# Weight slots requested from a recorded plan, first uses cast into the rings, and norm chains placed behind FFN matmuls, in a two-layer decoder trunk on eight cores

## The chip, the cores and the metric

The kernel runs as one program on all 8 cores of a Trainium2 chip. Each core takes half of one of the 4 sequences (4096 tokens and 128 more of overlap, 4224 in all), and no core waits for another. The time is device microseconds of the slowest core. Before the change it is 5761.13 us, the median of 6 runs from 5758.85 to 5765.34 us.

## The reference

Two layers; `d` is 1024, the FFN width 2816, the memory 256 tokens. Shortened from the reference:

```python
for l in range(2):
    x = x + 0.5 * swiglu(rms_norm(x, ffn1_norm[l]), gate1[l], up1[l], down1[l])      # F1
    h = rms_norm(x, mix_norm[l])
    q, k, v, u = split(h @ w_in[l])                          # 512 | 128 | 128 | 512 columns
    out_a = sliding_window_sink_attention(rope(q), rope(k), v, sinks[l])   # window 128, 8 heads
    out_b = multiscale_pool(u, pool_w[l], pool_scale[l])     # trailing means over 2, 4, 8, 16
    x = x + concat(rms_norm(out_a), rms_norm(out_b)) @ w_out[l]
    x = x + cross_attention(rms_norm(x), rms_norm(mem), wq[l], wkv[l], wo[l])   # 4 heads
    x = x + 0.5 * swiglu(rms_norm(x, ffn2_norm[l]), gate2[l], up2[l], down2[l])      # F2
return rms_norm(x, final_norm)
```

All weights arrive as f32 in HBM.

## The kernel before

The activations lie with the 1024 channels on the partitions (8 chunks of 128) and the tokens along the free dimension. The 4224 tokens are cut into nine tiles, six of 512 and three of 384, and each is passed twice, once for each layer: 18 passes. The main loop has 20 visits, `v` from -1 to 18. Visit `v` weaves three jobs together: F2 of pass `v-1`, the mixer and the cross attention of pass `v` (together M), and F1 of pass `v+1`. Visit -1 has F1 of pass 0 alone, visit 0 has no F2, visit 17 no F1, visit 18 only F2. In visits 0 and 9 M also prepares the memory (`memkv_steps`): it folds the memory's keys and values with `wq` and `wo` into eight slots `wab`, which the cross attention of the layer then reads.

The order of the work is written out by hand as lists of closures. `merge` weaves two lists by weights, `sprinkle` spreads one list evenly through another, and `run` calls the closures. Each call emits instructions to five in-order queues (PE, DVE, ACT, POOL, SP), and semaphores make one engine wait for another. In a visit with all three jobs the order is:

- gate and up of F2 (`gu2`, 22 pairs of 16 matmuls and an eviction), woven with the norm, the input projection and the pooling of M (`seg1`);
- down of F2 (`dn2`, 8 outputs of 22 matmuls), woven with the windowed attention (`seg2`) and with the norm that F1 needs (`prenorm_steps`); `seg2` ends with the norm of the attention's output (`ast.fin`, `anorm`);
- gate and up of F1 (`gu1`), woven with the output projection (`segw`);
- down of F1 (`dn1`): its first 72% with the cross attention (`seg4`), the rest with the norm for the next F2 (`tail`).

A norm is a chain over four engines: ACT squares a chunk, POOL adds it up, after the eighth chunk PE multiplies the sum by ones (`ps<-sb_ach,sb_ones` in the rows), ACT takes Ln and Exp (`sb_rst`), and DVE writes the scaled chunks into `sb_hF` or `sb_hM`, which PE then reads.

Weights come in slots of 128 x 2048 bf16 (512 KB; 16 matmuls of 512 columns use one) through two rings: F with six buffers (`sb_fr`), M with four (`sb_mr`). `load` issues a slot's DMA where the slot is first used in program order. The casts from f32 are DMAs of the POOL queue. The first use of F1's weights of layer 0 (`wf` 0, 33 slots, visit -1) casts straight into the ring, and SP writes the bf16 back to HBM (`wfb`). All other weights are first converted HBM to HBM: `conv_first` (the 9 slots of `wm` and the 16 of `wx`, layer 0) runs between visits -1 and 0, `conv_second` (`wf` 1) is sprinkled through visit 0, and layer 1's weights through visits 1 to 7.

The softmax here doesn't subtract the row's maximum and nothing guards it: scores larger than these inputs give would overflow.

## Time and profile before

| | |
|---|---|
| median of 6 runs | 5761.13 us |
| the profiled execution's own time | 5766.19 us |
| its span, first to last instruction, slowest core (core 6) | 5764.6 us |
| spans of all cores | 5731.9 to 5764.6 us |
| PE busy | 5175.1 us, 90% of the span |
| DVE, ACT, POOL busy | 2318.4, 1633.0, 937.1 us |
| HBM read, written | 1017.94 MB, 142.74 MB |
| chain that ended last | PE 75%, DVE 7%, DMA 7%, ACT 4%, issue 4% |

An engine's share is an average over visits with different limits, so the visits are looked at one by one. Their borders are read from the evictions of F1 and F2: visit -1 ends with the eighth down eviction at 265.6 us, visit 0 at 723.4 us, visit 1 at 1038.9 us. Where PE has no gap, an idle engine elsewhere costs nothing.

### The profile page before, as it was taken

What the parts mean: (1) busy time and instruction counts of PE and PEld (TensorE: products, weight loads), DVE (VectorE), ACT (ScalarE), POOL (GpSimd) and SP (SyncE); (2) the same over time, 40 slices, a digit from 0 to 9 for tenths busy, and PEclk for the clock granted to TensorE, in tenths of its full rate; (3) what the DMA queues carried; (4) which work ended last, traced back from release to release, by engine and by line L of the source; (5) the groups of instructions that cost most, each with busy time, mean ns of one, the idle gap of its engine ahead of it and who ended that gap; (6) DMA issues with size and microseconds to landing.
All of it is one profiled execution on the core that took longest, in us unless ns stands there. A gap on an engine that the chain in (4) does not pass through costs nothing.

```text
span 5764.6 us, 79056 instructions; the slowest of 8 cores (5731.9 to 5764.6 us)
## 1 busy us (share of the span) xinstructions
PE 5175.1 (90%) x25851; PEld 2493.6 (43%) x25851; DVE 2318.4 (40%) x3800; ACT 1633.0 (28%) x2824; POOL 937.1 (16%) x1015
## 2 busy tenths in 40 slices
PE   6436699999999999999999889999999999999988
PEld 2113244444444444455545434444444444455545
DVE  2122253444444443434434335353434444344452
ACT  1104232222323232222222333232232323232342
...
GB/s 192 124 149 162 170 174 202 154 200 150 189 162 181 170 194 176 198 211 230 201 188 160 178 174 142 162 136 179 132 176 136 167 143 173 161 187 182 196 157 165
DMA packets 254044, 991.79 MB, mean 172 GB/s; under 512 B 29264, under 2 KB 29664, under 8 KB 251008
## 3 DMA queue, kind: packets, MB, share of 16 engines
...
q10 hardware_dynamic: 1152, 2.10, 0.1%
...
HBM read 1017.94 MB, written 142.74 MB: 201 GB/s over the span
## 4 chain that ended last, share of the span: by engine, by line
PE 75%; DVE 7%; DMA 7%; ACT 4%; issue 4%; POOL 1%; another core or an unknown queue 1%; DVEq 0%; ACTq 0%; POOLq 0%; SPq 0%
PE ps L335 75%; DMA sb_fr<-wf 2%; DVE sb_hF L435 2%; DVE sb_hM L435 2%; DMA sb_fr<-wfb 1%; ACT sb_rst L148 1%; DMA wab<-sb_mr 1%; ACT sb_tmp L148 1%; DVE sb_x L523 1%; DMA sb_mr<-wmb 1%; DVE sb_hM L777 1%; DMA wfb<-sb_fr 1%; POOL sb_acc L407 1%; ACT sb_pT L148 1%
## 5 line engine op out<-in xcount | busy, mean ns | idle before, releaser
L335 PE MATMUL ps<-sb_hF,sb_fr 128*128 128x512 bf16 (+1 forms) x12672 | 2679.4, 367 | 172.2 <-DVE sb_hF L435 78.0
L335 PEld LDWEIGHTS ps<-sb_hF,sb_fr 128*128 128x128 bf16 x12672 | 1247.8, 99 | 1500.0 <-issue 303.3
L335 PE MATMUL ps<-sb_act,sb_fr 128*128 128x512 bf16 (+1 forms) x6336 | 1355.0, 366 | 95.3 <-DMA sb_fr<-wf 66.6
L487 DVE TENSOR_TENSOR sb_act<-ps,sb_sg 128x512 bf16<-128x512 f32 (+1 forms) x792 | 510.7, 645 | 1637.5 <-PE ps L335 1353.9
L407 POOL TENSOR_TENSOR sb_acc<-sb_acc,sb_sqf 128x512 f32<-128x512 f32 (+2 forms) x534 | 632.2, 1187 | 2482.6 <-ACT sb_sqf L148 2460.3
L335 PEld LDWEIGHTS ps<-sb_act,sb_fr 128*128 128x128 bf16 x6336 | 621.8, 99 | 760.1 <-issue 154.5
L335 PE MATMUL ps<-sb_hM,sb_mr 128*128 128x512 bf16 (+1 forms) x3600 | 832.5, 370 | 127.6 <-DMA sb_mr<-wmb 79.2
L148 ACT ACTIVATE sb_sg<-ps 128x512 f32<-128x512 f32 (+1 forms) x792 | 438.8, 558 | 1045.2 <-PE ps L335 909.9
L148 ACT ACTIVATE sb_sqf<-sb_x 128x512 f32<-128x512 f32 (+1 forms) x567 | 330.4, 591 | 991.1 <-DVE sb_x L825 432.9
L335 PEld LDWEIGHTS ps<-sb_hM,sb_mr 128*128 128x128 bf16 x3600 | 356.1, 99 | 539.4 <-issue 208.9
L148 ACT ACTIVATE sb_pT<-ps 128x512 bf16<-128x512 f32 (+2 forms) x436 | 232.3, 567 | 472.8 <-PE ps L335 472.1
L523 DVE SCALAR_TENSOR_TENSOR sb_x<-ps,sb_x 128x512 f32<-128x512 f32 (+1 forms) x288 | 183.9, 639 | 200.8 <-PE ps L335 200.7
L335 PE MATMUL ps<-sb_pT,sb_mr 128*128 128x512 bf16 (+2 forms) x1280 | 259.8, 354 | 3.2 <-DMA sb_mr<-wxb 3.0
L948 DVE TENSOR_TENSOR sb_pT<-sb_pT,sb_tmp 128x512 bf16<-128x512 bf16 (+1 forms) x144 | 103.4, 759 | 354.4 <-ACT sb_tmp L148 327.4
L435 DVE SCALAR_TENSOR_TENSOR sb_hF<-sb_x,sb_vecs,sb_rst 128x512 bf16<-128x512 f32 (+1 forms) x288 | 203.2, 761 | 46.4 <-ACT sb_rst L148 46.4
L435 DVE SCALAR_TENSOR_TENSOR sb_hM<-sb_x,sb_vecs,sb_rst 128x512 bf16<-128x512 f32 (+1 forms) x288 | 182.4, 701 | 55.9 <-ACT sb_rst L148 55.9
L976 DVE TENSOR_TENSOR sb_x<-ps,sb_x 128x512 f32<-128x512 f32 (+1 forms) x144 | 93.2, 647 | 273.0 <-PE ps L335 273.0
L407 POOL TENSOR_TENSOR sb_ach<-sb_acc,sb_sqf 128x512 bf16<-128x512 f32 (+1 forms) x101 | 118.8, 1176 | 409.3 <-ACT sb_sqf L148 295.2
L335 PEld LDWEIGHTS ps<-sb_pT,sb_mr 128*128 128x128 bf16 x1280 | 125.6, 98 | 123.1 <-issue 5.1
L148 ACT ACTIVATE sb_ubuf<-ps 128x512 f32<-128x512 f32 (+1 forms) x72 | 40.5, 562 | 413.0 <-PE ps L335 413.0
L335 PE MATMUL ps<-sb_ach,sb_ones 128*128 128x512 bf16 (+2 forms) x119 | 44.9, 378 | 124.7 <-POOL sb_ach L407 74.7
L148 ACT ACTIVATE sb_tmp<-sb_tmp 128x512 f32<-128x512 f32 (+1 forms) x204 | 125.6, 616 | 110.2 <-DVE sb_tmp L742 97.0
...
## 6 DMA issues: line engine op xcount, KB each, us to landing
sb_fr<-wfb SPq DMA_DIRECT2D x1155, 512.0 KB, 4.3
sb_mr<-wmb SPq DMA_DIRECT2D x162, 512.0 KB, 5.5
sb_mr<-wab SPq DMA_DIRECT2D x144, 512.0 KB, 4.3
...
sb_fr<-wf POOLq DMA_DIRECT2D x33, 512.0 KB, 15.4
wfb<-sb_fr SPq DMA_DIRECT2D x33, 512.0 KB, 11.5
...
sb_mr<-wxb SPq DMA_DIRECT2D x32, 512.0 KB, 4.2
```

What stands on the lines that cost most here:

```text
L148: return self.op("act", lambda h: h.activation(out=out, in_=in_, func=func, scale=scale, **kw), reads, writes)
L335: P.op("pe", lambda h: h.matmul(out_ap, lt, rh, start=st, stop=sp_, skip_group_check=True), reads=list(rb), writes=(ob_,), signal=(i == n ...
L407: P.op("pool", lambda h: h.tensor_tensor(out=o[:, :T], in0=acc[a][:, :T], in1=sqf[s][:, :T], op=ALU.add), (accb[a], sqfb[s]), (ob_,))
L435: P.op("dve", lambda h: h.scalar_tensor_tensor(out=out_ap, in0=in_ap, scalar=vcol(col), in1=r[0], op0=ALU.mult, op1=ALU.mult), (in_b, r[1] ...
L487: P.op("dve", lambda h: h.tensor_tensor(out=actF[:, hc, :T], in0=d[1][0][:, :T], in1=sg[si][:, :T], op=ALU.mult), (d[1][1], sgb[si]), (act ...
L523: P.op("dve", lambda h: h.scalar_tensor_tensor(out=x_, in0=pp[:, :T], scalar=0.5, in1=x_, op0=ALU.mult, op1=ALU.add), (ppb, xb_), (xb_,))
L777: P.op("dve", lambda h: h.scalar_tensor_tensor(out=hM[:, j, :T], in0=ao[:, j, :T], scalar=vcol(vb + 40 + j), in1=ast.r[0], op0=ALU.mult, o ...
L948: P.op("dve", lambda h: h.tensor_tensor(out=pT[:, pi_, :T], in0=pT[:, pi_, :T], in1=tmp[i][:, :T], op=ALU.mult), (pTb[pi_], tmpb[i]), (pTb ...
L976: P.op("dve", lambda h: h.tensor_tensor(out=x_, in0=pp[:, :T], in1=x_, op=ALU.add), (ppb, xb_), (xb_,))
```

## The change

In words:

- The builder runs twice. The first run records the order in which each ring takes slots (`plan`). In the second, `advance` issues the DMAs of later slots when a slot is taken: up to 4 positions ahead in F, up to 3 in M.
- `route` decides for each use whether the slot is cast from f32 by POOL and whether SP writes it back: `wf` 0 slots 0 to 16 are cast in visit -1 without a write-back and once more in visit 0 with one; slots 17 to 32 as before; `wf` 1 (visit 1) and `wm` of layer 0 (visit 0) are cast into the rings and written back; `wx` of layer 0 is cast and never written back. `conv_first` and `conv_second` are gone. Layer 1's conversions start in visit 2.
- The first norm is computed with eight accumulating matmuls by ones (`first_norm`) behind the first casts; tile 0 is loaded by SP and ACT in turn.
- `head_steps`, `tail_steps` and a new order at the start of `gu1` place the norm chains so that FFN matmuls stand between a chain's matmul by ones and the first matmul that reads its result.
- Constants get buffers (and so waits) of their own.

The core of the diff:

```diff
+KEEP = 17
...
+        AHEAD = {"F": NFR - 2, "M": NMR - 1}
+
+        def route(kind, a, s, occ):
+            if kind == "wf" and a == 0:
+                if occ == 0:
+                    return True, s >= KEEP
+                if occ == 1 and s < KEEP:
+                    return True, True
+            elif kind == "wf" and a == 1 and occ == 0:
+                return True, True
+            elif kind == "wm" and a == 0 and occ == 0:
+                return True, True
+            elif kind == "wx" and a == 0:
+                return True, False
+            return False, False
+
+        def advance(rk, ahead):
+            n = len(rings[rk])
+            while issued[rk] < len(plan[rk]) and issued[rk] <= pos[rk] + ahead:
+                p = issued[rk]
+                e = plan[rk][p]
+                i = p % n
+                if e is not None:
...
+                    if route(*e)[0]:
+                        P.dma("pool", slot[:, :], src[a, s], writes=(sb_,), box=swbox[rk][i])
+                    else:
...
+                        P.dma("sp", slot[:, :], dst[a, s], reads=rd, writes=(sb_,))
+                issued[rk] += 1
...
         def load(rk, kind, a, s):
-            i = ring_slot(rk)
-            slot, sb_ = rings[rk][i], ringb[rk][i]
...
+            i, e = step_ring(rk, (kind, a, s))
+            if route(*e)[1]:
+                src, dst, buf = BANKS[kind]
+                P.dma("sp", dst[a, s], rings[rk][i][:, :], reads=(ringb[rk][i],), writes=(buf[a][s],), box=wbbox[rk][i])
+            return rings[rk][i], ringb[rk][i]
...
-            seg2.append((lambda: None, 0.7))
-            seg2.append((ast.fin, 0.7))
-            seg2.append((lambda: anorm(0), 0.5))
-            seg2.append((lambda: anorm(2), 0.5))
+            seg2n = [ast.fin, lambda: anorm(0), lambda: anorm(2)]
...
+        def tail_steps(dn, xa, tail):
+            xs_ = raw(xa[:5])
+            out = raw(dn[:1]) + xs_[:1] + raw(dn[1:3]) + xs_[1:2] + raw(dn[3:4]) + xs_[2:4] + raw(dn[4:6]) + xs_[4:]
+            rest = dn[6:]
+            k = len(rest) - 9
+            out += merge(rest[:k], xa[5:])
+            t = raw(tail)
+            r = raw(rest[k:])
+            out += r[:1] + t[:1] + r[1:3] + t[1:2] + r[3:4] + t[2:3] + r[4:6] + t[3:4] + r[6:7] + t[4:] + r[7:]
+            return out
...
-                fs += sprinkle(merge(dn2, seg2), raw(ps_ + ph_))
-                fs += raw(gu1[:2])
...
+                ds = merge(dn2, seg2)
+                fs += sprinkle(ds[:len(ds) * 2 // 3], raw(ph_)) + ds[len(ds) * 2 // 3:]
+                cov = [f for f, w in gu1[:6] if w > 0]
+                evs = [f for f, w in gu1[:6] if w == 0]
+                fs += cov[:2]
...
+                fs += seg2n[:1] + fin2 + cov[2:] + seg2n[1:2] + evs[:1] + seg2n[2:] + evs[1:]
+                fs += merge(gu1[6:], final_steps(*F2) + [(lambda v=v: load_x(v + 2), 0.1)] + segw + seg3 + ropes)
+                fs += tail_steps(dn1, seg4, tail)
                 run(sprinkle(fs, bg))
             elif v == -1:
+                advance("F", AHEAD["F"])
+                first_norm()
...
-                run(conv_first)
```

Three places in the instruction order. The first is POOL at the start of the program (`sb_fr<-wf` is a cast into the F ring, `sb_acc` and `sb_ach` the sums of the first norm). Before:

```order
L407 TENSOR_TENSOR sb_acc<-sb_acc,sb_sqf 128x512 x6
L407 TENSOR_TENSOR sb_ach<-sb_acc,sb_sqf 128x512
L158 DMA sb_fr<-wf 128x2048
L158 DMA sb_maskc<-maskc 128x512
L158 DMA sb_maskp<-maskp 128x512
L158 DMA sb_poolw<-poolw 128x1024
L158 DMA sb_tmp<-posr 128x512
L158 DMA sb_fr<-wf 128x2048 x21
```

POOL at the same place with the change:

```order
L159 DMA sb_fr<-wf 128x2048 x9
L159 DMA sb_x<-xT 128x8x512
L159 DMA sb_maskc<-maskc 128x512
L159 DMA sb_maskp<-maskp 128x512
L159 DMA sb_poolw<-poolw 128x1024
L159 DMA sb_tmp<-posr 128x512
L159 DMA sb_fr<-wf 128x2048 x17
```

The seven additions are gone from POOL, nine casts stand first, and tile 1 follows them instead of standing behind the 22nd cast.

The second is PE in visit 11, from the end of `dn2` into `gu1` (`sb_act` is the down input, `sb_vtm` the windowed attention's values). Before:

```order
L335 MATMUL ps<-sb_pT,sb_vtm 64x512 x4
L335 MATMUL ps<-sb_pT,sb_ones 64x512 x4
L335 MATMUL ps<-sb_act,sb_fr 128x512 x22
L335 MATMUL ps<-sb_ach,sb_ones 128x512
L335 MATMUL ps<-sb_hF,sb_fr 128x512 x16
L335 MATMUL ps<-sb_ach,sb_ones 128x512
L335 MATMUL ps<-sb_hF,sb_fr 128x512 x96
```

PE there with the change:

```order
L343 MATMUL ps<-sb_pT,sb_vtm 64x512 x4
L343 MATMUL ps<-sb_pT,sb_ones 64x512 x4
L343 MATMUL ps<-sb_act,sb_fr 128x512 x11
L343 MATMUL ps<-sb_hF,sb_fr 128x512 x16
L343 MATMUL ps<-sb_ach,sb_ones 128x512 x2
L343 MATMUL ps<-sb_hF,sb_fr 128x512 x104
```

Between the last attention matmul and the matmul by ones stand 27 matmuls instead of 22, and both norms of the border now share one place.

The third is PE in the same visit, from the cross attention's norm to its last products (`sb_hM,sb_mr` are its scores, `sb_pT,sb_ones` its denominators, `sb_pT,sb_mr` its output). Before, its start and the denominator of the fourth head:

```order
L335 MATMUL ps<-sb_ach,sb_ones 128x512
L335 MATMUL ps<-sb_act,sb_fr 128x512 x11
L335 MATMUL ps<-sb_hM,sb_mr 128x512 x16
...
L335 MATMUL ps<-sb_pT,sb_ones 128x512 x2
L335 MATMUL ps<-sb_act,sb_fr 128x512 x11
L335 MATMUL ps<-sb_pT,sb_mr 128x512 x8
```

The same two pieces with the change, and the last rows before the next visit:

```order
L343 MATMUL ps<-sb_ach,sb_ones 128x512
L343 MATMUL ps<-sb_act,sb_fr 128x512 x44
L343 MATMUL ps<-sb_hM,sb_mr 128x512 x24
...
L343 MATMUL ps<-sb_pT,sb_ones 128x512 x2
L343 MATMUL ps<-sb_pT,sb_mr 128x512 x16
...
L343 MATMUL ps<-sb_pT,sb_mr 128x512 x24
L343 MATMUL ps<-sb_act,sb_fr 128x512 x11
L343 MATMUL ps<-sb_ach,sb_ones 128x512
L343 MATMUL ps<-sb_act,sb_fr 128x512 x55
```

Behind the norm's matmul by ones stand 44 FFN matmuls instead of 11; the 11 between the fourth head's denominator and the output products are gone, and the last norm is followed by 55.

## Rows read from the trace of the kernel before

**Rows 1.** Stretches (--windows): the visits, with their columns named first.

```profile
core 6: us, PE busy (x) PEld busy (x) DVE busy (x) ACT busy (x) POOL busy (x), PEclk, DMA share, GB/s
0.00:143.70 143.70, 86.57 (x353) 34.94 (x353) 29.18 (x55) 23.24 (x37) 26.92 (x43) 0.95 0.88 192
143.70:265.60 121.90, 55.41 (x179) 20.99 (x180) 11.83 (x16) 11.49 (x18) 21.44 (x22) 0.71 0.53 131
265.60:395.00 129.40, 18.21 (x65) 6.89 (x63) 12.96 (x27) 4.91 (x7) 5.88 (x10) 0.58 0.96 118
395.00:723.40 328.40, 228.06 (x1050) 103.90 (x1050) 104.25 (x166) 108.42 (x176) 57.03 (x68) 0.82 0.70 173
723.40:1038.90 315.50, 304.57 (x1418) 135.58 (x1418) 138.14 (x218) 88.36 (x147) 47.46 (x47) 0.99 0.62 180
...
3074.80:3427.60 352.80, 312.61 (x1637) 158.51 (x1637) 131.70 (x214) 113.72 (x203) 62.71 (x69) 0.95 0.52 176
3745.50:4063.10 317.60, 306.24 (x1419) 136.12 (x1419) 137.04 (x208) 92.98 (x155) 56.11 (x55) 0.98 0.44 152
...
5494.30:5661.40 167.10, 144.35 (x862) 82.12 (x862) 80.52 (x154) 77.03 (x122) 26.55 (x30) 0.97 0.45 151
```

**Rows 2.** Waits of PE, 0 to 723.4 us: total, times, longest.

```profile
PE ps L335 <- DMA sb_fr<-wf: 99.1, 25, 21.1
PE ps L335 <- DMA sb_mr<-wmb: 79.2, 2, 53.8
...
PE ps L335 <- DMA sb_fr<-wfb: 32.4, 1, 32.4
```

**Rows 3.** Chain of waits, 195 to 235 us: start, us, what.

```profile
195.89 5.89 DMA sb_fr<-wf
...
201.91 3.59 PE ps L335 x8
...
208.46 6.20 DMA sb_fr<-wf
```

**Rows 4.** Chain of waits, 270 to 400 us.

```profile
286.39 39.99 DMA sb_mr<-wmb
```

**Rows 5.** DMA queues, 60 to 130 us: packets, MB, share of 16 engines.

```profile
q0 software_dynamic: 2100, 7.66, 73.4%
q1 hardware_dynamic: 2104, 7.64, 28.8%
```

**Rows 6.** DMA queues, 1 to 13 us (tile 0).

```profile
q10 hardware_dynamic: 1152, 2.10, 66.6%
```

**Rows 7.** Chain of waits, unbroken PE in a 512 and a 384 visit.

```profile
4341.80 31.04 PE ps L335 x143
...
5221.78 23.41 PE ps L335 x143
```

**Rows 8.** Waits of PE in visit 11, 3745.5 to 4063.1 us.

```profile
PE ps L335 <- DVE sb_hF L435: 4.6, 6, 3.2
PE ps L335 <- DVE sb_ach L766: 3.2, 1, 3.2
PE ps L335 <- DVE sb_hM L435: 1.7, 6, 0.3
```

**Rows 9.** Waits of PE, 1700 to 2900 us.

```profile
PE ps L335 <- DMA sb_fr<-wfb: 20.4, 4, 5.8
```

**Rows 10.** Groups, visit 11: line, operation, count, busy, mean ns, idle before.

```profile
L407 POOL TENSOR_TENSOR sb_acc<-sb_acc,sb_sqf 128x512 f32<-128x512 f32 x32 | 40.5, 1272 | 155.5 <-ACT sb_sqf L148 155.4
...
L148 ACT ACTIVATE sb_tmp<-sb_tmp 128x512 f32<-128x512 f32 x12 | 7.5, 627 | 4.6 <-DVE sb_tmp L742 3.8
...
L948 DVE TENSOR_TENSOR sb_pT<-sb_pT,sb_tmp 128x512 bf16<-128x512 bf16 x8 | 6.2, 822 | 21.6 <-ACT sb_tmp L148 21.6
```

**Rows 11.** DMA issues, 3660 to 3977 us: count, KB, us to landing.

```profile
sb_fr<-wfb SPq DMA_DIRECT2D x66, 512.0 KB, 3.6
sb_mr<-wmb SPq DMA_DIRECT2D x9, 512.0 KB, 5.6
sb_mr<-wab SPq DMA_DIRECT2D x8, 512.0 KB, 3.8
```

More of the change, by code:

```diff
@@ L343, in mmw @@
             return n * (T / 2400.0 + 0.003)
-        fresh = set()
-        def flush_wb(rk, keep):
-            lst = pend_wb[rk]
-            while len(lst) > keep:
-                i, dst, buf = lst.pop(0)
-                P.dma("sp", dst, rings[rk][i][:, :], reads=(ringb[rk][i],), writes=(buf,), box=wbbox[rk][i])
-        def ring_slot(rk):
-            i = nxt("ring" + rk, len(rings[rk]))
-            while any(e[0] == i for e in pend_wb[rk]):
-                flush_wb(rk, len(pend_wb[rk]) - 1)
-            return i
@@ new lines, in advance @@
+        def advance(rk, ahead):
[5 more added lines that the diff above has]
+                if e is not None:
+                    kind, a, s, occ = e
+                    src, dst, buf = BANKS[kind]
+                    slot, sb_ = rings[rk][i], ringb[rk][i]
+                    if route(*e)[0]:
+                        P.dma("pool", slot[:, :], src[a, s], writes=(sb_,), box=swbox[rk][i])
+                    else:
+                        rd = tuple(buf[a][4:]) if kind == "wab" and s >= 4 else (buf[a][s],)
+                        if p > pos[rk] and not record and any(b_.w is None for b_ in rd):
+                            break
+                        P.dma("sp", slot[:, :], dst[a, s], reads=rd, writes=(sb_,))
+                issued[rk] += 1
@@ new lines, in _build, with step_ring @@
+        seen = {}
+        def step_ring(rk, key):
+            p = pos[rk]
+            e = None
+            if key is not None:
+                e = key + (seen.get(key, 0),)
+                seen[key] = e[3] + 1
+            if record:
+                plan[rk].append(e)
+            assert plan[rk][p] == e
+            advance(rk, 0 if e is None else AHEAD[rk])
+            assert issued[rk] > p
+            pos[rk] += 1
+            return p % len(rings[rk]), e
+        def ring_slot(rk):
+            return step_ring(rk, None)[0]
@@ L933, in den_mm @@
                 d[("pd", hd)] = (pd, pdb)
-                mm_group(pd[:, :T], pdb, [(ones[:, :], pT[:, d[(hd, mc)], :T], (constb, pTb[d[(hd, mc)]])) for mc in range(2)])
+                mm_group(pd[:, :T], pdb, [(ones[:, :], pT[:, d[(hd, mc)], :T], (onesb, pTb[d[(hd, mc)]])) for mc in range(2)])
             def den_act(hd):
@@ L1010, in build_program, with first_norm @@
             P.op("dve", lambda h: h.memset(ucarL[l][:, :, :], 0.0), writes=(ucarLb[l],))
-        P.act(esink[:, :], esink[:, :], AF.Exp, (sinkb,), (sinkb,))
+        def first_norm():
+            T = tiles[0][1]
+            key = ("f1", 0, 0)
+            st = Stat(NCH, D, T)
+            stats[key] = st
+            for c in range(NCH):
+                x_, b_ = xt(0, 0)[c]
+                if c % 2:
+                    P.op("dve", lambda h: h.tensor_tensor(out=pT[:, c, :T], in0=x_, in1=x_, op=ALU.mult), (b_,), (pTb[c],))
+                else:
+                    P.act(pT[:, c, :T], x_, AF.Square, (b_,), (pTb[c],))
+            st.ps = ps_next()
+            for c in range(NCH):
+                mm_group(st.ps[0][:, :T], st.ps[1], [(ones[:, :], pT[:, c, :T], (onesb, pTb[c]))], first=(c == 0), final=(c == NCH - 1))
+            st.fin_act()
+            P.act(esink[:, :], esink[:, :], AF.Exp, (sinkb,), (sinkb,))
+            run(raw(h_steps(0, 0, key, hF, hFb, 0)))
         def late_consts():
-            for (dst, src) in ((maskc, maskc_d), (maskp, maskp_d), (poolw, poolw_d)):
-                P.dma("pool", dst[:, :], src, writes=(constb2,))
+            for (dst, src, b_) in ((maskc, maskc_d, mkb[0]), (maskp, maskp_d, mkb[1]), (poolw, poolw_d, plwb)):
+                P.dma("pool", dst[:, :], src, writes=(b_,))
         def run(lst):
```

106 lines of the change are left out of this document (55 added, 51 removed).

## Prediction

> **What bounds the kernel now.** I read the stretches by visit first, then PE's waits in each, then the DMA queues where PE waits for DMA, then the chain of waits for the durations of single links. The reader is to see two different kernels. In visits -1 and 0 (to 723.4 us) PE is busy for 86.57 + 55.41 + 18.21 + 228.06 = 388 us, and the DMA engines are at 0.88, 0.53, 0.96 and 0.70 [rows 1]. What PE waits for there is casts, converted slots and reloads [rows 2]. In the middle of visit -1, casts and write-backs together take 73.4% + 28.8% of the DMA engines: they are full [rows 5]. In its second half they are not; there one cast follows another only after the previous result has passed PE, DVE, ACT and POOL, 12.6 us from cast to cast [rows 3]. Then PE stands for the conversions between the visits, 40 us in one piece [rows 4]. From visit 1 on PE is the bound: 306.24 us of 317.6, granted clock 0.98, and the waits that are left lie at the norms [rows 1, 8]. So the head is worth hundreds of us, and each later visit no more than its gap.
>
> That gap: unbroken, a matmul of 512 columns takes 31.04 / 143 = 0.217 us, one of 384 columns 0.164 us [rows 7]. Visit 11 has 1419, 32 of them with 128 columns (a quarter, about 0.06): 1387 x 0.217 + 2 = 303 us. The visit takes 317.6, so 14.6 us are open: 3.2 + 4.6 + 1.7 = 9.5 in waits [rows 8], the rest in the half clock that follows them (0.98 of 317.6 us is 6 us).
>
> **Prices of a slot.** 7.66 MB in 70 us are 14.6 slots of 0.524 MB: 70 x 0.734 / 14.6 = 3.5 us of full DMA for a cast, and 70 x 0.288 / 14.6 = 1.4 us for a write-back, also taken for a bf16 load [rows 5].
>
> The Trainium skill (DMA: Bandwidth & Descriptors, Specifications) gives about 358 GB/s of HBM for a core. By it a cast's 1.05 MB of f32 would take 2.9 us, an estimate from that page; the row's 3.5 decides, and with 2.9 the 80 casts of visits -1 and 0 would cost 48 us less.
>
> **Visit -1 (265.6 us before).** Its DMA work now: 33 casts 115.5, 16 write-backs 22.4, tile 0 8.0 (66.6% of 12 us [rows 6]), tile 1 5.6 (four slots' bytes at 1.4), constants and tables 3.5 (1.3 MB): 155 us. The casts start at once, not behind the first norm, and down's casts are issued four positions before their use, ahead of the additions that held POOL, so I take the engines as full throughout. With the last slot's matmuls (16 x 0.217 = 3.5), the eviction and the start: 162 us. Seventeen write-backs are gone here but come back in visit 0. PE's own 528 x 0.217 = 115 us is hidden behind this; with a first norm that ends near 25 us (an estimate: tile 0's 8 us of DMA beside five or six casts of 3.5) it is the lower bound, 140. The upper: every slot at 4.9, a start of 25 us, tiles and constants 17, so 204. I take 162, near the rows of the full engines.
>
> **Visit 0 (457.8 before).** The 129.4 us of conversions with PE at 18.21 [rows 1] go; their bytes do not. DMA now: 47 casts (17 `wf` 0, 9 `wm`, 16 `wx`, the first 5 of `wf` 1) 164.5; 58 bf16 transfers (26 write-backs, 16 reloads, `wab` 8 written and 8 read) 81; tile 2, memory, tables 10: 256 us. PE: visit 11's 303 without F2's 528 matmuls (115), plus the memory's 352.8 - 317.6 = 35 [rows 1]: 223. They don't overlap evenly. By the order, the last 281 matmuls (61 us) have 17 bf16 transfers and 5 casts beside them, 41 us, so PE is the bound there; before it stand 215 us of DMA against 162 of PE, and DMA is. That makes 215 + 61 = 276. What is late next: when the memory is folded, only the next slot is under way, since every other ring position is an output; a cast takes 6 us [rows 3] against some 3 us of matmuls, eight times: 24 us. And the first `wm` cast queues on POOL behind five F casts that wait for PE: 4 us. Sum 304. Bounds: 223 (PE alone) and 344 (the 328.4 us that the same matmuls took beside the conversion of `wf` 1 [rows 1], and 15 for the `wm` casts).
>
> **Visit 1 (315.5).** Its first half now casts `wf` 1: 28 casts 98, 33 write-backs 46, 5 M loads 7, 151 us, beside 680 matmuls, 148 us. About level: 0, between -10 and +12. Together the head gains (265.6 - 162) + (457.8 - 304) = 257 us.
>
> **The loads ahead, from visit 2 on.** I cost them at nothing. A slot asked for four positions ahead is still the buffer of the slot two positions back: its DMA waits until PE is done with that, so it starts five slots before its use. Before, the load stood at its use but SP ran ahead of PE until the buffer six positions back was free: five slots too. So the 20.4 us in which PE waited for F loads beside conversions [rows 9] stay; bounds 0 and 40, since visits 2 to 7 now hold up to five conversions instead of four. The wait that is added is M's: the load three ahead waits for the M slot just finished, and F's next loads queue behind it on SP. What covers it is four F slots, 14 us at least, against landings of 3.6 to 5.6 us [rows 11].
>
> **The norm chains.** Four places, by the order, per 512 visit:
> - End of the attention into `gu1`. Before, 22 matmuls (4.8 us) and a wait of 3.2: the chain took 8.0, since DVE also wrote `sb_hF` there. Now 27 matmuls, 5.9 us, and DVE free of that; four to six links of about 0.7 us are 4.2. I take 0.5 left. The 3.2 us wait for `sb_hF` itself [rows 8] goes: it is written in the first two thirds of `dn2`.
> - Norm of the cross attention: 44 matmuls, 9.5 us, before the first reader instead of 11. Eight DVE writes at 0.75 and Ln, Exp at 0.63 are 7.3: covered.
> - Last norm: its sum is now covered by 11 matmuls (2.4) instead of 22. DVE 0.7, ACT 0.63, POOL 1.27 [rows 10] are 2.6, with hand-overs 3.0: a new wait of 0.6. Its result has 55 matmuls: covered.
> - Fourth head: the 11 between denominator and output are gone. Ln, Exp (0.63 each) and DVE (0.82) [rows 10] are 2.1, with hand-overs 2.5, and the seventh product needs it after 1.3: 1.2, and 0.5 for its second half. New: 1.7.
>
> So 2.8 of the 14.6 us stay, and I take 12 us for each of visits 2 to 8 and 10 to 16, 15 visits: 180 (bounds 4 and 14.6 each). In the 384 visits cover and chain shrink together, as both go by columns. Visit 9 has 40 us open [rows 1], mostly the memory's own latencies: 12. Visit 17 has 862 x 0.164 = 141 us of matmuls in 167.1 [rows 1], but its cross attention stands without FFN matmuls between now: 10. Visit 18 is unchanged. Sum 202.
>
> **Sum.** 257 + 202 = 459. The profiled execution took 5766.2 us (1.6 outside the span): 5307. It lies 5.1 above the median of the runs, so 5302.
>
> **Rivals.**
> 1. The DMA engines are not kept full, because POOL issues the casts in order with its additions, copies and `wab` stores: visits -1 and 0 at their upper bounds, 204 and 344, 82 us more: 5384. For it: cast to landing serialized once already [rows 3]. Against: four positions of lead. Chance 18%.
> 2. The norm waits come back at the new places (the sums behind 11 and 16 matmuls): 4 us a visit instead of 12, 15 x 8 = 120: 5422. For it: the fourth head above. Chance 12%.
> 3. The head hides better: visit -1 at 145, visit 0 at 245: 76 us less, 5226. For it: 0.53 of DMA share in the second half before, so much room. Chance 11%.
> 4. Slower: on SP, F's loads behind an M load that waits for PE start only when that slot is done. Place: all 17 M loads of a visit [rows 11]. Price: up to a whole landing, 3.6 us, so 17 x 3.6 = 61 us in each of 17 visits, 1040: 6342. It decides from 459 / 289 = 1.6 us per M load. Against it: four F slots of cover. Chance 3%.
> 5. Slower: with fewer gaps TensorE gets less clock. If a visit had the 0.82 of 395 to 723 us instead of 0.98, its 303 us would be 59 us longer, 16.5 times: 6275. Against: at 96% busy the rows show 0.98 [rows 1], and what is missing from 1 there follows waits. Chance 2%. The Trainium skill (TensorE: Matmul & The Clock Gate, Seeing it yourself) speaks of a limit of 13/16 when three cores of a die run dense matmuls; no stretch of this trace shows it while eight cores run dense.
>
> The forecast has 54%.
>
> **How the numbers follow.** Predicted 5302. The range 5215 to 5410 takes in the forecast with its bounds, rivals 1 and 3 and the near half of rival 2; what stays out is the rest of 2 and of 3, and 4 and 5, some 15 to 20%. A measurement of this kernel tells 0.2% (12 us) from no change. Slower takes rivals 4 and 5, less the part of 4 that would end near zero: 4%; same 1%; faster 95%.
>
> **What would show it.** Visit -1's last down eviction near 162 us and visit 0's near 466, with a DMA share above 0.9 until some 400 us; no conversion between them; cast rows of 3.5 us. Visits 10 to 13 at 304 to 307 us, without a wait for `sb_hF`, and new short waits of PE for `sb_pT` by L948's successor and for `sb_ach`. I am wrong if visit 0 still takes 350 us or more, or if the 512 visits stay above 312 us.

## The result, and the profile after

The changed kernel takes 5435.12 us, the median of 10 runs from 5426.63 to 5439.02 us; the kernel before, run beside it, 5765.18 us (20 runs). The ratio is 0.9425, 95% interval 0.9417 to 0.9433. The forecast was 5302 us with a range to 5410: the change makes the kernel faster, by three quarters of what was forecast, and the time lies outside the range. The profiled execution took 5431.15 us, its slowest core (core 5) 5429.6 us. In some executions of the experiments below some cores run for long stretches at a granted clock of 0.81; times and visits are taken from executions and cores without that.

A visit's time runs from the eighth down eviction of one visit to that of the next, as before. The stretches of the changed kernel on core 5, which answer to [rows 1] and have its columns: visit -1; visit 0 in four pieces; visits 1 and 11.

```profile
0.00:167.30 167.30, 127.49 (x537) 53.04 (x537) 44.18 (x75) 32.66 (x51) 41.30 (x61) 0.98 0.96 189
167.30:250.00 82.70, 51.87 (x243) 23.11 (x244) 39.35 (x70) 15.22 (x23) 18.21 (x28) 0.84 1.02 213
250.00:400.00 150.00, 105.07 (x532) 52.27 (x530) 38.68 (x64) 62.69 (x105) 25.87 (x36) 0.83 0.77 173
400.00:450.00 50.00, 22.17 (x66) 7.88 (x66) 1.38 (x2) 10.08 (x17) 10.66 (x17) 0.69 0.47 111
450.00:541.50 91.50, 63.67 (x274) 26.91 (x273) 38.78 (x57) 23.41 (x37) 23.49 (x24) 0.85 0.39 114
541.50:863.00 321.50, 302.34 (x1418) 134.63 (x1417) 139.91 (x217) 89.72 (x147) 60.48 (x71) 0.99 0.80 207
3478.40:3782.70 304.30, 299.33 (x1421) 135.38 (x1420) 137.84 (x206) 94.04 (x155) 58.53 (x55) 1.00 0.49 160
```

The reader is to see two things. Visit 11 is what was forecast: 304.3 us, PE busy for 299.33 of it, granted clock 1.00 against 0.98 before. And in visit 0 the DMA engines are full for 83 us only; from 400 us on they are at 0.47 and 0.39, and PE is busy for 22.17 of 50 us there. Against the forecast, slowest core by slowest core:

| visits | before | after | gain | forecast |
|---|---|---|---|---|
| -1 | 266 | 168 | 98 | 103.6 |
| 0 | 458 | 374 | 84 | 153.8 |
| 1 | 316 | 322 | -6 | 0 |
| 2 to 8 | 2036 | 1978 | 58 | 84 |
| 9 | 353 | 333 | 20 | 12 |
| 10 to 16 | 2067 | 1987 | 80 | 84 |
| 17, 18 | 258 | 256 | 2 | 10 |
| all | | | 335 | 447.4 |

The forecast's own sum was 459: it multiplied 12 us by 15 visits, where 2 to 8 and 10 to 16 are 14.

What PE waits for in visit 0, 167.3 to 541.5 us, answering to [rows 2] (total us, times, longest; the four largest):

```profile
PE ps L343 <- DMA sb_mr<-wx: 37.3, 6, 12.5
PE ps L343 <- DVE sb_hM L476: 26.7, 4, 22.8
PE ps L343 <- DMA sb_mr<-wm: 17.7, 1, 17.7
PE ps L343 <- POOL sb_ach L448: 15.6, 2, 14.7
```

Casts of `wx` come late again and again, the first of `wm` by 17.7 us, and the input of the cross attention (`sb_hM`) by 22.8 us in one piece.

In visit 11, which answers to [rows 8], two waits are left, both at places that the forecast named (the sums of the norms, and the fourth head):

```profile
PE ps L343 <- POOL sb_ach L448: 3.6, 2, 1.9
PE ps L343 <- DVE sb_pT L986: 1.4, 2, 1.1
```

### The profile page after: what moved, and what is told of

It is laid out like the page before. It is cut to its first block, busy times and chain, and to the rows that moved or that the text cites. A ratio compares the mean times of both kernels' runs of the same rounds, so it can differ in the third digit from the quotient of the medians.

```text
span 5429.6 us, 79466 instructions; the slowest of 8 cores (5401.1 to 5429.6 us)
## 1 busy us (share of the span) xinstructions
PE 5074.0 (93%) x25858; PEld 2481.1 (46%) x25858; DVE 2333.8 (43%) x3804; ACT 1645.9 (30%) x2816; POOL 980.5 (18%) x1065
## 4 chain that ended last, share of the span: by engine, by line
PE 80%; DMA 11%; DVE 3%; ACT 2%; issue 2%; POOL 1%; DVEq 0%; ACTq 0%; POOLq 0%; SPq 0%
PE ps L343 80%; DMA sb_fr<-wfb 3%; DMA sb_fr<-wf 3%; DMA wfb<-sb_fr 2%; DMA wab<-sb_mr 2%; ACT sb_tmp L149 1%; POOL sb_ach L448 1%; DMA sb_mr<-wx 1%; ACT sb_sqf L149 1%; POOL sb_acc L448 0%; ACT L146 0%; DVE sb_pT L986 0%; DMA sb_x<-xT 0%; DMA sb_ao<-memT 0%; DMA sb_mr<-wm 0%
## 5 line engine op out<-in xcount | busy, mean ns | idle before, releaser
L343 PE MATMUL ps<-sb_hF,sb_fr 128*128 128x512 bf16 (+1 forms) x12672 | 2627.3, 364 | 71.1 <-DMA sb_fr<-wfb 37.6
L343 PE MATMUL ps<-sb_act,sb_fr 128*128 128x512 bf16 (+1 forms) x6336 | 1327.1, 363 | 22.7 <-DMA sb_fr<-wf 16.5
L343 PE MATMUL ps<-sb_hM,sb_mr 128*128 128x512 bf16 (+1 forms) x3600 | 784.1, 364 | 48.3 <-DVE sb_hM L476 25.5
L564 DVE SCALAR_TENSOR_TENSOR sb_x<-ps,sb_x 128x512 f32<-128x512 f32 (+1 forms) x288 | 184.6, 641 | 285.7 <-PE ps L343 284.6
L476 DVE SCALAR_TENSOR_TENSOR sb_hF<-sb_x,sb_vecs,sb_rst 128x512 bf16<-128x512 f32 (+1 forms) x288 | 227.3, 841 | 11.5 <-ACT sb_rst L149 11.5
L1014 DVE TENSOR_TENSOR sb_x<-ps,sb_x 128x512 f32<-128x512 f32 (+1 forms) x144 | 93.1, 647 | 184.3 <-PE ps L343 184.3
L448 POOL TENSOR_TENSOR sb_ach<-sb_acc,sb_sqf 128x512 bf16<-128x512 f32 (+2 forms) x100 | 116.6, 1166 | 303.5 <-PE ps L343 159.3
L863 DVE TENSOR_TENSOR sb_x<-ps,sb_x 128x512 f32<-128x512 f32 (+1 forms) x144 | 92.6, 643 | 138.4 <-PE ps L343 138.4
L652 DVE TENSOR_TENSOR sb_tmp<-ps,sb_sin 64x512 f32<-64x512 f32 (+1 forms) x180 | 116.0, 644 | 47.4 <-PE ps L343 35.6
```

Source lines behind the costliest of these rows:

```text
L343: P.op("pe", lambda h: h.matmul(out_ap, lt, rh, start=st, stop=sp_, skip_group_check=True), reads=list(rb), writes=(ob_,), signal=(i == n ...
L448: P.op("pool", lambda h: h.tensor_tensor(out=o[:, :T], in0=acc[a][:, :T], in1=sqf[s][:, :T], op=ALU.add), (accb[a], sqfb[s]), (ob_,))
L476: P.op("dve", lambda h: h.scalar_tensor_tensor(out=out_ap, in0=in_ap, scalar=vcol(col), in1=r[0], op0=ALU.mult, op1=ALU.mult), (in_b, r[1] ...
L564: P.op("dve", lambda h: h.scalar_tensor_tensor(out=x_, in0=pp[:, :T], scalar=0.5, in1=x_, op0=ALU.mult, op1=ALU.add), (ppb, xb_), (xb_,))
L652: P.op("dve", lambda h: h.tensor_tensor(out=t1[lo:lo + 64, :T], in0=pp[hi:hi + 64, :T], in1=sinS[pr][lo:lo + 64, :T], op=ALU.mult), (ppb, ...
L863: P.op("dve", lambda h: h.tensor_tensor(out=x_, in0=pp[:, :T], in1=x_, op=ALU.add), (ppb, xb_), (xb_,))
```

## Experiments

**What was disputed.** (GpSimd is POOL in the rows, ScalarE ACT, VectorE DVE.) Theory: the 70 us missing in visit 0 are waits in GpSimd's in-order queue, where casts, the stores of `wab`, the norms' additions and the tables' transfers stand behind one another. Rival: the DMA engines have more to do than was counted. A third question was whether the gain from visit 2 on comes from the borders or from the loads ahead.

The theory's place is seen on POOL itself. Its timeline in visit 0 of the changed kernel, 405 to 490 us (start, us, instruction, in brackets the idle time before it and what ended that):

```profile
413.65 0.70 POOL L159 DMA_DIRECT2D wab<-sb_mr  x1 [2.03 <-DMA wab<-sb_mr]
416.83 0.67 POOL L159 DMA_DIRECT2D wab<-sb_mr  x1 [2.48 <-DMA wab<-sb_mr]
419.50 0.67 POOL L159 DMA_DIRECT2D wab<-sb_mr  x1 [2.00 <-DMA wab<-sb_mr]
420.09 0.65 POOL L159 DMA_DIRECT2D sb_mr<-wx  x1
...
465.32 0.64 POOL L159 DMA_DIRECT2D sb_tmp<-posr  x1
474.00 1.32 POOL L448 TENSOR_TENSOR sb_acc<-sb_acc,sb_sqf 128x512 f32<-128x512 f32 x1 [8.04 <-ACT sb_sqf L149]
```

Four stores write one ring slot out in quarters, one into each of four slots of `wab`, and the program counts them as writers of one buffer, so each waits until the one before has landed. The cast of the next `wx` slot is issued behind the third of these waits, and the position load of the rotary tables (`sb_tmp<-posr`) behind the last store. Over 372 to 490 us POOL's waits for landings sum to:

```profile
POOL wab L159 <- DMA wab<-sb_mr: 42.5, 12, 7.0
```

The late position load is also what the 22.8 us wait for `sb_hM` goes back to, through two more in-order queues. The same core's rows, in order of time:

```profile
457.28 0.38 PE L343 MATMUL ps<-sb_ach,sb_ones 128*128 128x512 bf16 x1
468.53 0.43 DVE L597 CAST sb_sin<-sb_tmp 128x512 f32<-128x512 int32 x1 [53.64 <-DMA sb_tmp<-posr]
473.22 0.63 ACT L149 ACTIVATE sb_sqf<-sb_x 128x512 f32<-128x512 f32 x1 [25.80 <-DVE sb_x L564]
485.06 0.69 ACT L149 ACTIVATE sb_rst<-ps,sb_vecs 128x512 f32<-128x512 f32 x1
487.58 0.59 PE L343 MATMUL ps<-sb_hM,sb_mr 128*128 128x512 bf16 x1 [22.80 <-DVE sb_hM L476]
```

The cross attention's norm has its sum on PE at 457.28 us. Its Ln on ACT (`sb_rst`) comes at 485.06, behind the square of an F1 output and the tables' two sines (475.96 and 482.41 us). That square waits for an F1 eviction on DVE (L564), and the eviction stands behind the tables' first steps, which start when the position load has landed. The addition on POOL at 474.00 us belongs to the next norm; the expectations of e3 and e12 below take it for this one.

The runs in one table: means of the visits over the cores of the profiled execution, in us (cores 4 to 7 in e1 and e6, 0 to 3 in e3, all eight in the others), and the lowest time of the run. e6 has no time that can be compared; e5 and e10 come below.

| kernel | visit -1 | visit 0 | 2 to 8 | 9 | 10 to 16 | lowest time |
|---|---|---|---|---|---|---|
| before | 260.7 | 454.5 | 2027.8 | 354.4 | 2066.2 | 5758.85 |
| after | 166.6 | 371.2 | 1967.4 | 335.5 | 1985.8 | 5426.63 |
| e1, stores apart | 169.6 | 344.2 | 1973.8 | 323.1 | 1987.4 | 5415.92 |
| e2, memory load early | 169.8 | 361.9 | 1976.6 | 333.2 | 1987.0 | 5445.92 |
| e3, tables early | 170.6 | 347.6 | 1976.3 | 335.4 | 1986.7 | 5414.43 |
| e4, KEEP 0 | 190.8 | 344.3 | 1981.4 | 335.3 | 1987.4 | 5444.67 |
| e5b, nothing ahead | 211.6 | 497.7 | 1964.3 | 336.8 | 1986.2 | 5678.79 |
| e6, borders of before | 169.9 | 370.7 | 2044.3 | 350.8 | 2069.7 | - |
| e7, four conversions | 171.1 | 370.5 | 1946.5 | 335.4 | 1987.2 | 5415.73 |
| e8, `wm` earlier | 183.4 | 352.1 | 1979.6 | 335.3 | 1986.6 | 5435.30 |
| e9, e1+e2+e3+e7+e8 | 182.3 | 317.6 | 1947.1 | 323.9 | 1986.2 | 5364.33 |
| e11, tables by ScalarE | 180.2 | 306.8 | 1948.7 | 322.2 | 1986.8 | 5355.67 |
| e12, that alone | 170.8 | 356.9 | 1984.7 | 335.9 | 1987.8 | 5441.33 |
| e13, e11 by GpSimd | 182.8 | 314.5 | 1949.0 | 324.0 | 1987.4 | 5367.35 |

How much the same code scatters can be read from the kernels that leave a visit as it was: visit -1 stands at 166.6 to 171.1 us (the changed kernel is the lowest of seven), visit 0 at 370.5 to 371.2 (three), visits 2 to 8 at 1964.3 to 1984.7 (eight) and 10 to 16 at 1985.8 to 1987.8. So a single edit is read from its own visit, not from the whole time.

**e4: no first half kept back (`KEEP` 0).** All casts of `wf` 0 are written back in visit -1, so visit 0 has 17 casts less.

```diff
-KEEP = 17
+KEEP = 0
```

> KEEP 0 instead of 17: all 33 slots of wf 0 are written back in visit -1 and reloaded as bf16 in visit 0, so visit 0 has 17 x (4.9 - 1.4) = 60 us less DMA work and visit -1 has 17 x 1.4 = 24 us more. If full DMA engines set visit 0 (the prediction's sum), it falls from 374 to about 315 us and the whole to about 5400. If POOL's in-order queue and the chains behind it set it, only the stretch of visit 0 in which the engines are full (its first 80 us) gains, 10 to 20 us, visit -1 grows by 15 to 24, and the whole stays at 5430 to 5450.

The two visits on core 1 (columns as above):

```profile
0.00:188.90 188.90, 130.80 (x542) 53.21 (x543) 44.61 (x77) 32.65 (x51) 39.38 (x57) 0.95 1.00 217
188.90:527.80 338.90, 239.48 (x1110) 109.46 (x1108) 117.93 (x195) 111.49 (x181) 71.17 (x91) 0.85 0.60 150
```

By the shares, visit 0 now takes 338.9 x 0.60 = 203 us of full engines; in the changed kernel it takes 82.7 x 1.02 + 150 x 0.77 + 50 x 0.47 + 91.5 x 0.39 = 259. With 56 us less for the engines the visit is 27 us shorter on the mean of the cores, between the 10 to 20 of the queue theory and the 59 of the rival, and visit -1 pays 20 to 24 back. Most of the gain lies before the memory's part: PE's wait for the first `wm` cast falls from 17.7 to 3.1 us on this core, those for `wx` (34.0) and `sb_hM` (24.1) are about what they were. At a mean share of 0.60 the engines do not hold the visit as a whole, and still it stands at 344: the rival's size is wrong. The forecast's amount of DMA (256 us) was right.

**e1: each quarter store a buffer of its own** (the stores' line; the list of buffers and the wait of the reloads of `wab` follow it).

```diff
-P.dma("pool", dv[:, s, :, h, :], sv[:, s, :, :], reads=(ob_,), writes=(wabuf[l][4 + h],), box=abbox[d["o"]])
+P.dma("pool", dv[:, s, :, h, :], sv[:, s, :, :], reads=(ob_,), writes=(wabB[l][h][s],), box=abbox[d["o"]])
```

> The four stores of a head's output slot into wab get a buffer each, so that POOL no longer waits for one to land before it issues the next (12 waits of some 2 us in a layer, and in visit 0 the casts queued behind them). Queue theory: the stretch from the first output matmul of the memory's second half to its last (406 to 446 us) shrinks by 15 to 25 us in visit 0, visit 9 by up to 5; the whole about 5412. Full-engines theory: nothing, 5435. Third: the casts' own landing of 7 us for each head holds it, then 5 us or less.

POOL of core 5 in e1, 400 to 470 us:

```profile
409.83 2.82 POOL L159 DMA_DIRECT2D wab<-sb_mr  x4 [7.78 <-ACT sb_mr L149]
412.11 1.10 POOL L159 DMA_DIRECT2D sb_mr<-wx  x1
```

Four stores go out in 2.8 us instead of one every 2.7 to 3.2, and the cast follows at once. Visit 0 is 27 us shorter, where the theory said 15 to 25, and visit 9, which folds the second layer's memory in the same code, 12, where it said 5 at most. On core 5 PE's waits for `wx` fall to 22.1 us, and those for `sb_hM` to 12.4, since the position load is issued earlier as well.

**e3: the rotary tables ahead of the output projection.** Their transfers then stand on POOL before the memory's.

```diff
-ms = rest[1] + seg2 + mid + segw + [(f_, 2 * w_) for f_, w_ in seg3] + ropes
+ms = rest[1] + seg2 + mid + ropes + segw + [(f_, 2 * w_) for f_, w_ in seg3]
```

> In visit 0 the rotary tables of tile 1 are made before the output projection instead of behind the memory's steps. Queue theory: the cross attention's norm waits because its additions stand on POOL behind the tables' position load and stores, so the hole from 446 to 488 us closes by 20 to 28 us; the whole about 5410. Full-engines theory: nothing, 5435. If the norm itself is late, for its own chain, the hole moves to its additions and less than 8 us are gained.

Visit 0 is 24 us shorter. PE of core 0 there:

```profile
PE ps L343 <- DMA sb_mr<-wx: 37.6, 5, 13.4
...
PE ps L343 <- DVE sb_hM L476: 2.8, 3, 2.0
```

The wait for `sb_hM` falls from 26.7 to 2.8 us, that for `wx` stays: two separate things behind one queue.

**e2: the load of the memory earlier.**

```diff
+if v == 0:
+    ms = rest[1] + seg2 + mid[1:] + seg3[:1] + mid[:1] + segw + [(f_, 2 * w_) for f_, w_ in seg3[1:]] + ropes
```

> In visit 0 the memory is loaded right behind the attention's norm, before the output projection, instead of behind it. The load took 10.6 us on the chain of waits at 320 us. Queue theory: the hole from 317 to 345 us closes by 8 to 11 us (the eight additions on POOL behind it, 6 us, can then run beside the projection too, 17 at most); the whole 5420 to 5427. Full-engines theory: nothing.

Visit 0 is 9 us shorter, as the queue theory said (8 to 11). On core 7 PE's waits for sums from POOL shrink to 5.6 us (15.6 in the changed kernel), and those for `wm` grow to 26.4 (17.7): part of what is gained comes back one cast earlier.

**e8: the first casts of `wm` asked for in visit -1.**

```diff
                 run(merge(gu, extra))
+                advance("M", AHEAD["M"])
```

> The first four casts of wm (layer 0) are issued on POOL between gate/up and down of visit -1 instead of at M's first step in visit 0. Queue theory: the 17.7 us wait of PE for the first of them, which stands behind F casts that wait for PE, goes; first M matmul some 20 us after the visit's start instead of 41; visit -1 3 to 10 us longer, for their 14 us of DMA; net 10 to 20 us, the whole about 5420. Full-engines theory: the same bytes earlier, so what visit 0 gains visit -1 loses, net 0.

Visit 0 is 19 us shorter, and PE's waits there for `wm` are gone or, on some cores, down to 4 us. Visit -1, where the engines are full, is 17 us longer than in the changed kernel and 12 to 14 longer than in the other kernels that leave it alone. So the net is 2 to 7 us and not the 10 to 20 of the queue theory: where the engines are at 0.96, an earlier cast mostly moves the time, as the rival said.

**e5 and e5b: nothing asked for ahead of its use.**

```diff
-AHEAD = {"F": NFR - 2, "M": NMR - 1}
+AHEAD = {"F": 0, "M": 0}
```

> AHEAD is 0 in both rings: each slot's DMA is issued at its own use in program order, all else as changed. The prediction's reasoning on the rings: from visit 2 on SP runs ahead of PE anyway and a load starts five slots early either way, so visits 10 to 16 stay within 1 us; visits -1 and 0 lose, since a cast then stands on POOL behind additions that wait for PE: visit -1 from 168 to 220 or more, visit 0 by 30 or more, the whole 5500 to 5560. Rival: the loads ahead do give lead in the full visits; then each of 10 to 16 loses 3 us or more.

> AHEAD 0 in both rings once more, for the visits -1 to 5, which ran at a granted clock of 0.81 in the execution profiled before: visit -1 some 225, visit 0 between 420 and 500, visit 1 between 340 and 430, visits 2 to 5 as changed (302 to 306), the whole 5600 to 5700. If visits 2 to 5 stay above 310 at full clock, the loads ahead do count beside conversions.

e5b is the kernel of e5 once more, and its rows are used here. The lowest times are 5676.28 us (e5) and 5678.79 (e5b), above the 5500 to 5560 expected of e5. Visits -1, 0, 1 and 4 of e5b on core 1:

```profile
0.00:213.40 213.40, 139.26 (x537) 56.07 (x537) 45.26 (x77) 32.42 (x51) 38.65 (x57) 0.88 0.72 147
213.40:713.70 500.30, 270.17 (x1108) 116.26 (x1108) 118.42 (x195) 111.59 (x181) 78.12 (x104) 0.75 0.46 113
713.70:1119.50 405.80, 329.44 (x1423) 140.92 (x1424) 138.68 (x219) 89.71 (x147) 63.26 (x75) 0.90 0.63 169
1421.90:1724.00 302.10, 298.98 (x1420) 135.14 (x1418) 140.94 (x219) 89.59 (x147) 48.42 (x47) 1.00 0.67 188
```

Without the lead the casts cost (211.6 - 166.6) + (497.7 - 371.2) + (398.9 - 319.8) = 251 us in visits -1 to 1, the last pair being visit 1. From 0 to 1100 us PE waits there for casts, which POOL issues: 152.3 us for `sb_fr<-wf`, 81.9 for `sb_mr<-wx`, 55.3 for `sb_mr<-wm`. For the reloads `sb_fr<-wfb`, which SP issues, it waits 6.0. From visit 2 on nothing is lost: 1964.3 against 1967.4 us in visits 2 to 8, 1986.2 against 1985.8 in 10 to 16. The lead is worth what it gives to transfers that POOL issues; those that SP issues had it already.

**e6: the steady order of before, with the new loads.** `head_steps`, `tail_steps` and the new start of `gu1` undone, for instance:

```diff
-fs += tail_steps(dn1, seg4, tail)
+d1, d2 = split_frac(dn1, 0.72)
+fs += merge(d1, seg4)
+fs += merge(d2, tail)
```

> The visits 1 to 16 take the order of before (norm chains where they were), with the loads ahead, the casts into the rings and the order of visits -1, 0 and 17 as changed. If the gain from visit 2 on is the borders alone, visits 10 to 13 go back from 304.3 to 317 to 318 us and the whole to about 5590 to 5600. If the loads ahead carry part of it, they stop below 315 us.

PE in visit 11, core 7, the three largest waits:

```profile
PE ps L343 <- DVE sb_hF L476: 4.6, 6, 3.2
PE ps L343 <- DVE sb_ach L807: 3.4, 1, 3.4
PE ps L343 <- DVE sb_hM L476: 1.7, 6, 0.3
```

These are the waits of [rows 8], and visits 10 to 16 take 2069.7 us, as before. The borders are worth 84 us there, 77 in visits 2 to 8, and 14 to 15 each in visits 1 and 9. In visits 2 to 8 the kernel with the old borders is 16 us slower than before: something else there costs (e7). In visit 1 it stands at 333.8 us, 18 above before.

**e7: conversions of layer 1 over visits 2 to 9, four in each.** The changed kernel has them in visits 2 to 7, five in each.

```diff
-k = -(-len(conv_later) // max(1, ntl - 1 - v))
+k = -(-len(conv_later) // max(1, ntl + 1 - v))
```

> Layer 1's 29 conversions are spread over visits 2 to 9, four in a visit, instead of 2 to 7, five in a visit. Theory: two conversions that POOL issues 20 us apart (1951.6 and 1972.1 us) hold back the F loads behind them and make the waits of 12.1 and 8.2 us of visit 5; with four in a visit visit 5 falls from 305.6 to about 290 and visits 2 to 7 together lose 15 to 25 us, visits 8 and 9 gain at most 5. Rival: the loads wait whenever any conversion runs, whatever their number in a visit; then the waits move to other visits and the sum stays within 5 us.

Visits 2 to 8 are 21 us shorter than in the changed kernel, and the rival's 5 us are out: they stand at 1946.5 to 1949.0 us in the four kernels with four conversions (e7, e9, e11, e13) and at 1964.3 or more in those with five. The ratio to before is 0.9387, interval 0.9347 to 0.9428. In visit 5 of the changed kernel PE waits for F's reloads (1778 to 2085 us):

```profile
PE ps L343 <- DMA sb_fr<-wfb: 23.2, 3, 12.1
```

Three of the transfers issued there, 1948 to 1998 us (queue, count, KB each, median us to landing):

```profile
sb_fr<-wfb SPq DMA_DIRECT2D x7, 512.0 KB, 34.3
wxb<-wx POOLq DMA_DIRECT2D x1, 2048.0 KB, 25.7
wfb<-wf POOLq DMA_DIRECT2D x1, 1536.0 KB, 21.4
```

Two conversions 20 us apart, and a reload takes 34.3 us against 3.6 [rows 11]: more than the lead. Over visits 2 to 8 these waits sum to 41.1 us in the changed kernel and to 25.9 with four a visit (core 2 of e7):

```profile
PE ps L343 <- DMA sb_fr<-wfb: 25.9, 9, 11.3
```

**e9 and e10: the edits together.** e9 has e1, e2, e3, e7 and e8; e10 has e1, e2, e3, e7 and `KEEP` 0.

> Five edits together: a buffer for each store of wab, memory load and rotary tables ahead of the output projection in visit 0, the first wm casts in visit -1, four conversions a visit. If visit 0 is a sequence of chains through POOL, each of which was taken away by itself (30, 22, 5 to 17, 22 us), the gains add up: visit 0 from 374 to 290 to 305 us, near the 304 of the prediction, visit -1 182, visit 9 some 323, visits 2 to 7 25 us less; the whole 5310 to 5335. If they are several readings of one wait, visit 0 stops at 335 to 345 and the whole at 5360 or above.

> As e9_all, with KEEP 0 in place of the first wm casts in visit -1 (the two did the same for the first M matmul, and KEEP 0 also takes 60 us of DMA work out of visit 0 for 24 in visit -1). If the engines bind visit 0 once the chains are gone, visit 0 falls below 285 us and the whole under that of e9_all by 5 to 15; if not, visit -1's 189 us make it equal or slower by up to 10.

e9 takes 5364.33 and 5366.19 us. Its visit 0 (317.6) lies between the 290 to 305 of adding up and the 335 to 345 of one wait; the whole time is where the latter had it. It has a new wait, on core 2 (PE's waits, then DVE's timeline):

```profile
PE ps L344 <- DVE sb_act L529: 22.2, 3, 20.3
```

```profile
313.12 0.43 DVE L598 CAST sb_sin<-sb_tmp 128x512 f32<-128x512 int32 x1 [28.72 <-DMA sb_tmp<-posr]
```

With the tables early, VectorE's table work waits for the position load that POOL has issued late, and the evictions stand behind it. In e10 visits -1 and 0 take 494 to 503 us together on cores 0, 1, 6 and 7, and in e9 492 to 508: `KEEP` 0 adds nothing.

**e11: the tables at their place, their transfers on ScalarE's queue** (with e1, e2, e7 and e8).

```diff
-P.dma("pool", posi[:, :T], posr_d[:, c0:c0 + T], writes=(tmpb[3],))
+P.dma("act", posi[:, :T], posr_d[:, c0:c0 + T], writes=(tmpb[3],))
...
-P.dma("pool", tab_d[ti, j, :, :T], tb[:, :T], reads=(bb,), writes=(tabbuf[ti][j],), box=tabbox[pr * 2 + j])
+P.dma("act", tab_d[ti, j, :, :T], tb[:, :T], reads=(bb,), writes=(tabbuf[ti][j],), box=tabbox[pr * 2 + j])
```

> The changed kernel with four of the single edits of e9 (own buffers for the conversions' stores, memory's casts earlier, the first four casts of wm in visit -1, four conversions a visit up to visit 9), and the rotary tables left at their place in visit 0, but their position load and their stores issued from ScalarE's queue instead of GpSimd's. Theory (GpSimd's queue in order is the cause of visit 0's last hole): with the position load and the stores off it, the x norm's additions and memory's casts no longer stand behind them, visit 0 comes to 285 to 305 us, and the whole to 5335 to 5360 us. Rival (the wait only changes its engine, as in e9, where PE waited 20.3 us for an activation tile behind the tables' work on VectorE): visit 0 stays at 315 us or more, and the whole at 5365 us, like e9, or slower.

Visit 0 comes to 302 to 310 us, on the mean 2 above the theory's 285 to 305, and the whole to 5355.67 us. What PE still waits for in visit 0 (core 4, the four largest):

```profile
PE ps L344 <- DMA sb_mr<-wx: 21.6, 4, 7.5
PE ps L344 <- DVE sb_ach L808: 10.6, 1, 10.6
PE ps L344 <- DMA sb_mr<-wm: 9.9, 2, 7.7
PE ps L344 <- DVE sb_hM L477: 9.4, 3, 7.8
```

**e12: that edit alone on the changed kernel; e13: e11 with it undone.**

> The changed kernel with one edit: the rotary tables' position load and their two stores are issued from ScalarE's queue instead of GpSimd's; their place in the program and all else stay. Theory (order in GpSimd's queue): PE's wait of 22.8 us for the cross attention's input before its norm's additions goes for the most part, and visit 0 comes from 366 to 374 us to 340 to 355 us. Rival (the tables' own work on ScalarE and VectorE is what the norm stands behind, whatever queue issues their transfers): visit 0 stays at 362 us or more.

> The kernel of e11 with the tables' transfers back on GpSimd's queue, the other three edits of visit 0 and the four conversions a visit kept. Theory (order in GpSimd's queue): visit 0 is 10 to 22 us longer than the 303 to 310 us of e11, with the norm of the cross attention's input late again. Rival (with the conversions' stores no longer waiting for one another, the queue runs ahead and the tables' place on it costs nothing): visit 0 stays within 5 us of e11.

e12's visit 0 is 352 to 361 us, 14 below the changed kernel, between theory and rival; e13's is 8 above e11's, between them too. PE's waits for `sb_hM` in visit 0, first e12 (core 0), then e13 (core 6):

```profile
PE ps L343 <- DVE sb_hM L476: 8.9, 3, 7.3
```

```profile
PE ps L344 <- DVE sb_hM L477: 16.0, 3, 14.3
```

So of the 22.8 us some 15 were the queue's order, and some 7 stay where the tables' work on ScalarE and VectorE stands before the norm. The rest of e3's 24 us was not split further. e13 takes 5367.35 and 5373.13 us, against the kernel before a ratio of 0.9314, interval 0.9274 to 0.9354. e11's 5355.67 us is the lowest time of the study; its next one is 5388.17, so whether it beats e13 as a whole program is open.

The Trainium skill (DMA: Bandwidth & Descriptors, Issuing engines are not separate DMA queues) says that DMAs issued from several engines save only the time in which a sequencer issues them. Here the three transfers, at 0.64 us of issue each at most, gave 8 to 14 us: what the move saved was the standing behind POOL's waits, so the measurement decides.

## Why the prediction was wrong

**The step that failed: visit 0 (154 us forecast, 84 measured).** It said: "before it stand 215 us of DMA against 162 of PE, and DMA is", with 24 us for the memory's casts and 4 for the first `wm` cast. The amount was right, 256 us forecast and 259 measured. Wrong was that the engines would be full for 215 us. They are full for 83; after that their share is 0.77, 0.47 and 0.39, and from 400 us on POOL's queue, which issues the transfers, stands between them. Of the late pieces two were named: the memory's casts, for which 24 us were taken and PE waits 37.3 (22.1 with the stores apart), and the first `wm` cast, taken at 4 and late by 17.7. The stores of `wab` and the tables were not named. The runs give the pieces of the 371.2 us: 27 for stores of `wab` that wait for one another (e1), 9 for the memory's place (e2), 8 to 14 for the tables' transfers on POOL (e12, e13), up to 24 with the tables' place (e3), and 19 for the first `wm` casts (e8), of which visit -1 takes 12 to 17 back. The first, second and last of these together (e13) give 57 us, 27 + 9 + 19 = 55 alone: they add. The tables' part overlaps with the stores', which delay the position load. With the tables as well (e11), visit 0 stands at 306.8, 3 us above the forecast, partly because visit -1 now does some of its work. Visits -1 and 0 together then take 487.0 us, where 466 were forecast and 537.8 measured; the last 21 us were not taken apart.

This was rival 1 in kind (18%), for visit 0 alone: its 204 for visit -1 did not come, and its 344 for visit 0 was too low, against 374. That bound was built from the 328.4 us row of before, taken as PE's work beside a conversion. But the row held the same stores. POOL of the kernel before, 570 to 660 us:

```profile
POOL wab L158 <- DMA wab<-sb_mr: 35.1, 12, 5.7
```

The prediction read PE's waits and not POOL's. PE's view shows a late cast; only the issuing engine's shows why it was late. The "40 us in one piece" that it read in [rows 4] are the landing of one slot; PE's longest wait there is 53.8 us [rows 2]. No term of the sum uses it.

Beside visit 0's 70 us, the forecast misses 26 in visits 2 to 8, 12 by the count of visits, and 9 because the profiled execution lay 5 us above the median before and 4 below it after.

**Visit -1 (104 forecast, 98 measured): right.** The share is 0.96 over 167 us, 161 us of full engines against 155 counted. The prices hold too. The DMA queues from 60 to 130 us, which answer to [rows 5] (packets, MB, share of 16 engines):

```profile
q0 software_dynamic: 2811, 10.05, 86.6%
q1 hardware_dynamic: 1081, 3.96, 16.2%
```

10.05 MB are 19.2 slots (the two table stores, one slot's worth, counted with them): 70 x 0.866 / 19.2 = 3.2 us for a cast, where 3.5 was taken, and 70 x 0.162 / 7.6 = 1.5 for a write-back. The estimate of 2.9 us for a cast from the figure of the Trainium skill (DMA: Bandwidth & Descriptors, Specifications) is approached and not reached. The first FFN matmul starts at 27.7 us, where a first norm that ends near 25 was estimated.

**Visit 1 (0, measured -6): the number right, in part by luck.** It lies within -10 to +12. But with the old borders (e6) the visit takes 333.8 us, 18 more than before, so the casts alone lie outside the range; the new borders, which the sum left out here, give 14 back. Its first half, 541.5 to 704 us, has a DMA share of 1.02 for 162.5 us, where 151 of DMA beside 148 of PE were counted.

**Loads ahead from visit 2 on (nothing): right,** by e5b. The bound beside it, "visits 2 to 7 now hold up to five conversions instead of four", was named and not priced: by e7 it is 21 us, most of the 26 that visits 2 to 8 lack.

**Norm chains (12 us a visit): right in place and size, two sums aside.** Visits 10 to 13 were forecast at 304 to 307 and take 304.2 to 304.3 us, 13 to 14 less than before, and by e6 all of it is the order at the borders. The wait of the fourth head was forecast at 1.7 and is 1.4 us; the sums' at 1.1, and they are 3.6, since two of them stay late by 1.7 to 1.9 us. Rival 2, which let them take most of it back, is out. The count of visits was wrong by one (12 us).

**Visits 9 and 17.** Visit 9 gives 20 instead of 12 us, 15 of them by the borders (e6). Visit 17 gives 2 instead of 10. The largest of PE's waits there is for the sum behind the attention (5161 to 5327 us):

```profile
PE ps L343 <- DVE sb_ach L807: 11.3, 1, 11.3
```

In the kernel before the same wait takes 8.1 us in visit 17; the forecast did not read it. Without a next F1 the new order has nothing to put behind the attention's last product; that this alone makes the difference was not tested.

**Rivals 3, 4 and 5.** Rival 3 (the head hides better) went the other way: the head gains 182 us, where 257 were forecast. Rivals 4 and 5 (SP's queue; a lower clock when PE has no gaps) are not seen. PE does not wait for an F load in visits 10 to 16, and the granted clock of visit 11 rose to 1.00.
